# First attention: keys and values for two heads from one weight chunk, four heads' made ahead, heads written out

## What is computed

```python
q, c_kv, k_rope, q_idx, k_idx, w_idx, q_mem = split_cols(h @ w_in, A_SPLITS)
# 8 heads of 128 (96 without, 32 with rotary positions), c_kv of rank 256, sequence 512
c_kv = rmsnorm(c_kv, kv_norm)
# in dsa_attention, by blocks of 128 queries:
dots = jnp.einsum('bqhd,bsd->bqhs', q_idx, k_idx)          # 16 indexing heads of 64
score = jnp.einsum('bqhs,bqh->bqs', jax.nn.relu(dots), w_idx)
_, idx = lax.top_k(jnp.where(causal, score, -inf), topk)   # 128 of at most 512 keys
s = (q_nope @ w_uk . c_kv[idx] + q_rope . k_rope[idx]) * scale
o = softmax(s) @ c_kv[idx]                                 # per head
out = einsum('bshr,rhv->bshv', o, w_uv)
```

## Time and profile before

| what | value |
|---|---|
| median of 3 runs | 2329.89 us (2325.2 to 2333.39) |
| profiled execution, its own time | 2322.4 us |
| its span, first to last instruction | 2320.6 us |
| mean granted TensorE clock | 0.973 of full |
| TensorE busy (matmuls) | 2196.7 us, 95% |
| VectorE busy | 1284.8 us, 55% |
| ScalarE busy | 879.0 us, 38% |
| GpSimd busy | 194.8 us, 8% |
| DMA issues of the weight stream | 334 of 512 KB, 3.5 us to landing |
| chain that ended last | TensorE 84%, VectorE 8%, issue 3%, ScalarE 3%, DMA 1% |

### The profile page before, as it was taken

The page is one execution under the profiler, slowest core; times in us unless marked ns, Lnnn a source line. Parts: engine busy times, 40 slices in busy tenths (PEclk is TensorE's granted clock), DMA queues, the critical chain, the costliest instruction groups (busy, mean ns, idle before and its releaser), DMA issues.

```text
span 2320.6 us, 32126 instructions
## 1 busy us (share of the span) xinstructions
PE 2196.7 (95%) x10706; PEld 1789.9 (77%) x10706; DVE 1284.8 (55%) x2274; ACT 879.0 (38%) x1654; POOL 194.8 (8%) x110
## 2 busy tenths in 40 slices
PE   7986999999999899999999999999999987999997
PEld 6675877888888778788888888888888765777776
DVE  5876444666644546556666445555554474366653
ACT  4443444333222246633333332222222354355541
POOL 0032220100001111110000121000000100000002
PEclk9997999999999999999999999999999998999989
DMA  3121111323333311123233333332332233200002
GB/s 136 54 82 55 64 64 46 100 90 99 99 99 101 92 44 37 37 82 99 91 100 98 104 102 96 97 99 92 97 99 91 90 109 100 64 19 19 19 10 73
DMA packets 50046, 182.90 MB, mean 79 GB/s; under 512 B 5552, under 2 KB 5680, under 8 KB 49840
## 3 DMA queue, kind: packets, MB, share of 16 engines
q1 hardware_dynamic: 49824, 181.35, 24.8%
q0 software_dynamic: 144, 0.52, 0.1%
HBM read 179.76 MB, written 2.10 MB: 78 GB/s over the span
## 4 chain that ended last, share of the span: by engine, by line
PE 84%; DVE 8%; issue 3%; ACT 3%; DMA 1%; POOL 0%; DVEq 0%; ACTq 0%; POOLq 0%; SPq 0%
PE pj L2030 69%; PE po L2316 3%; PE ps L2276 2%; PE po L2215 2%; PE ps L2169 2%; PE pt L2291 2%; ACT w_both L683 1%; PE pt L2185 1%; DVE w_both L1215 1%; DVE rtmp L1345 1%; PE pj L2140 1%; PE ps L2408 1%; DMA raw<-in_wstream 1%; DVE score L1785 1%; PE po L2224 1%
## 5 line engine op out<-in xcount | busy, mean ns | idle before, releaser
L2030 PE MATMUL pj<-h_hi,w_both 128*128 128x512 f32 x3472 | 1134.0, 399 | 26.3 <-DVE w_both L1215 18.8
L2030 PEld LDWEIGHTS pj<-h_hi,w_both 128*128 128x128 f32 x3472 | 657.9, 189 | 165.5 <-issue 17.2
L683 ACT ACTIVATE w_both<-raw 128x1024 fp32r<-128x1024 f32 x334 | 353.9, 1060 | 864.8 <-PE pj L2030 855.1
L2030 PE MATMUL pj<-h_lo,w_both 128*128 128x512 f32 x1736 | 680.4, 392 | 0.0
L1215 DVE TENSOR_TENSOR w_both<-raw,w_both 128x1024 fp32r<-128x1024 f32 x296 | 400.2, 1352 | 386.7 <-ACT w_both L683 386.4
L2030 PE MATMUL pj<-G_hi,w_both 128*128 128x512 f32 x1408 | 440.0, 393 | 3.1 <-DVE G_lo L1442 3.0
L2030 PEld LDWEIGHTS pj<-h_lo,w_both 128*128 128x128 f32 x1736 | 329.6, 190 | 63.9 <-issue 1.4
L2030 PEld LDWEIGHTS pj<-G_hi,w_both 128*128 128x128 f32 x1408 | 266.9, 190 | 63.1 <-DVE G_lo L1442 3.8
L2030 PE MATMUL pj<-G_lo,w_both 128*128 128x512 f32 x704 | 275.9, 392 | 0.0
L2030 PEld LDWEIGHTS pj<-G_lo,w_both 128*128 128x128 f32 x704 | 133.3, 189 | 27.3
L601 POOL TENSOR_TENSOR ssum<-sq 128x512 f32<-128x512 f32 x6 | 9.4, 1562 | 1396.7 <-ACT sq L892 1396.7
(11 more groups left out here) (315 smaller groups left out, 2395.2 us busy)
## 6 DMA issues: line engine op xcount, KB each, us to landing
raw<-in_wstream SPq DMA_DIRECT2D x334, 512.0 KB, 3.5
xT<-in_x SPq DMA_DIRECT2D x4, 512.0 KB, 9.4
out_x<-xT SPq DMA_DIRECT2D x4, 512.0 KB, 2.7
memT<-in_mem SPq DMA_DIRECT2D x1, 1024.0 KB, 12.5
cst<-in_cst SPq DMA_DIRECT2D x1, 512.0 KB, 10.7
tab<-in_tab POOLq DMA_DIRECT2D x1, 512.0 KB, 4.9
posi<-in_pos SPq DMA_DIRECT2D x1, 256.0 KB, 2.8
vec<-in_vec SPq DMA_DIRECT2D x1, 182.5 KB, 2.4
```

The source lines that it names most:

```text
L683: nc.scalar.activation(w_hi[:, c.par * CW:(c.par + 1) * CW], raw[:, c.par * CW:(c.par + 1) * CW], ACT.Copy).then_inc(hi_ready, 1)
L2030: mm = nc.tensor.matmul(acc, w[:, col:col + P], x[part], start=first and k == 0, stop=last and k == 2)
```

## The change

- The stage `aq` has 14 chunks instead of 18: q0, q1, kv0, kv1, q2, q3, q4, kv2, q5, q6, kv3, q7, q8, q9. A `kv` chunk has keys and values of two heads: 4 key blocks, and 4 value blocks in the order in which the two heads' 128 columns lie side by side. The number of uses of the `pj` banks stays 26 (a pair takes four).
- TensorE's `pair_keys` makes the keys of two heads (12 matmuls of 512 columns), `pair_values` their values in 24 matmuls of 256 columns, two token blocks to a bank.
- Pairs 0 and 1 (heads 0 to 3) and query 2 are made before the first scores. Pair 2 is made in head 2, pair 3 in head 4: keys at unit 0, values at unit 1. The query of head j + 3 is made in head j (j up to 6): in pieces of 6 matmuls at each unit, or of 9, 9 and 6 at units 1 to 3 in heads 2 and 4. Head 7 makes nothing.
- ScalarE takes each head's keys when they are done (`pair_done`), then the two halves of the values, and splits one chunk behind each pair and one behind each query. The keys' copies stand ahead of the exponential of unit 2, the values' copies and the split ahead of that of unit 3.
- `a_k` holds four heads and `a_v` two pairs, over memory that the indexing and `ckv` are done with; `rope_key` copies the rotated rows four times.
- `attention_tiles` has no hardware loop for `aq`.

```diff
@@ -38,7 +38,7 @@
 
-STAGES = [("afront", 2), ("idx", 8), ("ckv", 2), ("mem", 8), ("aq", 18), ("aout", OUT_CHUNKS), ("up0", 2 * FT),
+STAGES = [("afront", 2), ("idx", 8), ("ckv", 2), ("mem", 8), ("aq", 14), ("aout", OUT_CHUNKS), ("up0", 2 * FT),
           ("down0", DT * DOWN_CHUNKS), ("bfront", 4), ("bq", 8), ("bmem", 2), ("bout", OUT_CHUNKS), ("up1", 2 * FT),
@@ -58,6 +58,12 @@
           "nz0", "nz1", "cmp2", "nz2", "nz3", "nz4", "nz5", "nz6", "nz7"]
+AQ = ["q0", "q1", "kv0", "kv1", "q2", "q3", "q4", "kv2", "q5", "q6", "kv3", "q7", "q8", "q9"]
+AQ_TILE, _t = {}, 0
+for _name in AQ:
+    AQ_TILE[_name] = TL["aq"] + _t
+    _t += 4 if _name[:2] == "kv" else 1
+assert _t == dict(TILES)["aq"] and len(AQ) == dict(STAGES)["aq"]
 TAKES = {"c": 0, "cmp": 2}
@@ -323,7 +329,8 @@
 
-    a_k, a_v = put("a_k", 2 * S, at=g0 + 20 * KB), put("a_v", 2 * S, at=g0 + 24 * KB)
+    a_k = put("a_k", 4 * S, at=g0 + 20 * KB)
+    a_v = [put("a_v0", 2 * S, at=g0 + 36 * KB), put("a_v1", 2 * S, at=g1 + 38 * KB)]
     c_hi, c_lo = put("c_hi", 2 * S, f32r, at=g0 + 28 * KB), put("c_lo", 2 * S, f32r, at=g0 + 32 * KB)
@@ -514,6 +522,10 @@
 
+            if ph.name == "aq":
+                for j in range(ph.tiles):
+                    tile(ph, 0, j)
+                return
             tile(ph, 0, 0)
@@ -569,18 +581,13 @@
                 return At(CH[ph.name] + j, i, 2), At(TL[ph.name] + j, i, 2)
-            if isinstance(i, int) and j < 2:
-                return At(CH["aq"] + j), At(TL["aq"] + j)
-            if isinstance(i, int) and j == ph.tiles + 1:
-                return At(CH["aq"] + 17), At(TL["aq"] + 25)
-            return At(CH["aq"] + 2 * j, i, 4), At(TL["aq"] + 3 * j, i, 6)
-
-        def keys_values_at(i, j):
-
-            if isinstance(i, int) and j == 0:
-                return At(CH["aq"] + 2), At(TL["aq"] + 2)
-            return At(CH["aq"] + 1 + 2 * j, i, 4), At(TL["aq"] + 1 + 3 * j, i, 6)
-
+            return At(CH["aq"] + AQ.index(f"q{j}")), At(AQ_TILE[f"q{j}"])
+
+        def pair_at(n):
+
+            return At(CH["aq"] + AQ.index(f"kv{n}")), At(AQ_TILE[f"kv{n}"])
+
+        PAIR_IN = {2: 2, 4: 3}
 
@@ -741,12 +748,26 @@
 
-            def keys_values(i, j):
-
-                c, t = keys_values_at(i, j)
-                par = j % 2
-                take(a_k[0:96, par * S:(par + 1) * S], t, c, rows=slice(0, 96))
-                take(a_v[:, par * S:(par + 1) * S], t + 1, c)
+            def pair_keys(n):
+
+                t = pair_at(n)[1]
+                for hh in range(2):
+                    at = (n % 2 * 2 + hh) * S
+                    act.wait_ge(pair_done, 3 * n + hh + 1)
+                    nc.scalar.activation(a_k[0:96, at:at + S], pj[(t + hh).par][0:96, :],
+                                         ACT.Copy).then_inc(pj_free[(t + hh).par], 1)
+
+            def pair_values(n):
+
+                c, t = pair_at(n)
+                for part in range(2):
+                    if part:
+                        act.wait_ge(chunk_used, c.v + 3)
+                    else:
+                        act.wait_ge(pair_done, 3 * n + 3)
+                    nc.scalar.activation(a_v[n % 2][:, part * S:(part + 1) * S], pj[(t + part).par][:, :],
+                                         ACT.Copy).then_inc(pj_free[(t + part).par], 1)
+                split_hi(c + 2)
 
@@ -798,18 +819,16 @@
                         query(ph, i, j + 2)
-                    if ph.name == "aq" and u == 1 and more(ph, i, j):
-                        keys_values(i, j + 1)
+                    if ph.name == "aq" and j in PAIR_IN and u < 2:
+                        (pair_keys, pair_values)[u](PAIR_IN[j])
                     if u == ph.at_refill and more(ph, i, j):
 
-                        if ph.name == "aq":
-                            split_hi(keys_values_at(i, j + 1)[0] + 2)
-                        elif ph.name == "bmem" or ph.name != "amem" and not (isinstance(i, int) and j == 0):
+                        if ph.name == "bmem" or ph.name == "bq" and not (isinstance(i, int) and j == 0):
                             split_hi(query_at(ph, i, j + 1)[0] + 2)
                     softmax(ph, i, j, u + 2)
-                    if u == ph.at_query and ph.name == "aq":
-                        query(ph, i, j + 2)
-                        split_hi(query_at(ph, i, j + 2)[0] + 2)
+                    if u == ph.at_query and ph.name == "aq" and j < ph.tiles - 1:
+                        query(ph, i, j + 3)
+                        split_hi(query_at(ph, i, j + 3)[0] + 2)
                     last = before(ph, i, j, p)
@@ -821,8 +840,11 @@
                 if name == "aq":
-                    keys_values(0, 0)
-                    split_hi(keys_values_at(0, 0)[0] + 2)
+                    for n in range(2):
+                        pair_keys(n)
+                        pair_values(n)
+                    query(ph, 0, 2)
+                    split_hi(query_at(ph, 0, 2)[0] + 2)
                 if name == "bmem":
@@ -1724,8 +1746,8 @@
                 link(rope(ktmp[:, 0:S], vraw[:, :], tab128, SHUF128, t))
-                for par in range(2):
-                    nc.vector.tensor_copy(a_k[96:P, par * S:(par + 1) * S], ktmp[96:P, 0:S])
+                for slot in range(4):
+                    nc.vector.tensor_copy(a_k[96:P, slot * S:(slot + 1) * S], ktmp[96:P, 0:S])
 
@@ -2122,23 +2144,32 @@
 
-            def keys_values(i, j):
-
-                c, t = keys_values_at(i, j)
+            def pair_keys(n):
+
+                c, t = pair_at(n)
                 arrived(c)
-                free(t)
-                for k in range(2):
-                    product(pj[t.par][:, :], k, c.par, (c_hi[:, k * S:(k + 1) * S], c_lo[:, k * S:(k + 1) * S]),
-                            k == 0, k == 1)
-                free(t + 1)
-                acc = pj[(t + 1).par]
+                for hh in range(2):
+                    free(t + hh)
+                    for k in range(2):
+                        mm = product(pj[(t + hh).par][:, :], 2 * hh + k, c.par,
+                                     (c_hi[:, k * S:(k + 1) * S], c_lo[:, k * S:(k + 1) * S]), k == 0, k == 1)
+                    mm.then_inc(pair_done, 1)
+
+            def pair_values(n):
+
+                c, t = pair_at(n)
                 for b in range(NB):
+                    at = t + 2 + b // 2
+                    if b % 2 == 0:
+                        free(at)
                     for k in range(2):
-                        col = c.par * CW + (2 + k) * P
+                        col = c.par * CW + (4 + 2 * k) * P
                         here = slice(k * S + b * P, k * S + (b + 1) * P)
-                        for n, (x, w) in enumerate(((c_hi, w_hi), (c_hi, w_lo), (c_lo, w_hi))):
-                            mm = nc.tensor.matmul(acc[:, b * P:(b + 1) * P], x[:, here], w[:, col:col + P],
-                                                  start=k == 0 and n == 0, stop=k == 1 and n == 2)
+                        for m, (x, w) in enumerate(((c_hi, w_hi), (c_hi, w_lo), (c_lo, w_hi))):
+                            mm = nc.tensor.matmul(pj[at.par][:, b % 2 * 2 * P:(b % 2 + 1) * 2 * P], x[:, here], w[:, col:col + 2 * P],
+                                                  start=k == 0 and m == 0, stop=k == 1 and m == 2)
+                    if b == 1:
+                        mm.then_inc(pair_done, 1)
                 mm.then_inc(chunk_used, 1)
@@ -2152,13 +2183,13 @@
                     if branch in ("mem", "topk"):
-                        q = query_at(ph, i, j)[1] if branch == "mem" else keys_values_at(i, j)[1] + 1
+                        q = query_at(ph, i, j)[1] if branch == "mem" else pair_at(j // 2)[1] + 3
                         pe.wait_ge(pj_free[q.par], q.half + 2)
...
                 if branch == "topk":
-                    keys = a_k[:, par * S:par * S + w]
+                    keys = a_k[:, j % 4 * S:j % 4 * S + w]
                 elif branch == "mem":
@@ -2206,7 +2237,7 @@
                     if branch == "topk":
-                        val = a_v[:, j % 2 * S + kb * P:j % 2 * S + (kb + 1) * P]
+                        val = a_v[j // 2 % 2][:, (2 * kb + j % 2) * P:(2 * kb + j % 2 + 1) * P]
                     elif branch == "mem":
@@ -2234,11 +2265,13 @@
 
-                    if ph.name == "aq" and u == 0 and more(ph, i, j):
-                        keys_values(i, j + 1)
+                    if ph.name == "aq" and j in PAIR_IN and u < 2:
+                        (pair_keys, pair_values)[u](PAIR_IN[j])
                     if ahead(ph, i, j):
-                        if ph.name == "aq" and u:
-                            query(ph, i, j + 2, (range(0, 3), range(3, 6), range(6, CB))[u - 1])
+                        if ph.name == "aq" and j < ph.tiles - 1:
+                            pieces = ((), range(0, 3), range(3, 6), range(6, CB)) if j in PAIR_IN else (
+                                range(0, 2), range(2, 4), range(4, 6), range(6, CB))
```

(28 more changed lines are left out.)

1 line of the change is left out of this document (added).

## The result

The changed kernel took **2306.42 us** (median of 4 runs, 2304.8 to 2310.26) beside 2331.34 us for the kernel before (4 runs): ratio 0.990, 95% interval 0.9876 to 0.9923. The size of the gain, about 1%, is known less well than these medians make it look. With twelve executions of a later group the kernel before has 2324.4, 18.0 above 2306.42; in another group it has 2328.8 (15 executions), and the changed kernel, run again beside it, 2305.86: 22.9. The two profiled executions (2322.4 and 2305.13) are 17.3 apart. So the gain is 17 to 25 us, and the profiles account for the 17. Forecast were -15.6 and 2314.3, in a range of 2305 to 2325.

The account below looks back on a forecast made before the run. VectorE's top-k was taken to bound until about 211 us, TensorE after it. Thin heads -17.0, pair heads +4.9, last head -4.3 and key copies +0.8 give -15.6 us, from the median 2329.9 to 2314.3; range 2305 to 2325.

Parts of the forecast that it names:

- no new waits: Rival: rope and exponentials come in time in the heads, TensorE is the only bound; 2307.4 us, chance 0.12.
- The bound: First attention: VectorE's top-k bounds until about 211 us, TensorE after it.
- The front: Pairs 0, 1 and query 2 before the first scores end near 205 us, hidden by the top-k; first turn stays at 211.
- my sign of being wrong, "after 212": A first turn of the first attention after 212 us would show the forecast wrong.
- Thin heads: Heads 0, 1, 3, 5, 6 without key and value work: 4.0 less, 0.65 rope wait; -3.4 each, -17.0 us.
- Pair heads: Heads 2 and 4, each making a pair: +1.65 of matmuls and 0.8 of waits, +2.45 each, +4.9 us.
- The rival that 256 columns cost twice 128: Value matmuls save nothing by pairing: +2.4 in each of two pair heads, 2319.2 us, chance 0.05.
- The last head: Query work gone from the last head, up to the memory attention's first waiting score: -3.2 - 1.1 = -4.3 us.
- Key copies: Two more key copies of 0.42 us on VectorE at 80 us delay the top-k: +0.8 us.
- rope takes over: Rival: GpSimd's subtraction blocks both rope halves, 1.4 us more in five heads; 2321.3 us, chance 0.10.
- front not covered: Rival: TensorE stays at 1.2 GHz from 187 us, first turn at 219; +8, 2322.4 us, chance 0.10.
- clock drops in the thin heads: Rival: TensorE's clock drops at both waits of seven heads, 26 us slower; 2340 us, chance 0.04.

Follow-up runs that it names:

- rounds_ahead_before: Kernel before, with the product `rck` made by GpSimd and two top-k rounds moved ahead of the norm of `ckv`: 2317.08 us, ratio 0.9957.
- pair1_in_head0: Changed kernel with pair 1 made in head 0 instead of in front of the first scores: 2310.58 us, ratio 0.9935.
- rope_ahead: Changed kernel with VectorE roping query j + 2 in units 2 and 3 of head j, not query j + 1 in units 0 and 1: 2301.35 us.
- exp_first: Changed kernel with ScalarE's exponentials ahead of a pair's copies and split in heads 2 and 4: 2310.8 us, ratio 0.9921.
- before_again: Kernel before, not edited, run and profiled again: 2324.37 us, ratio 0.9991.
- all_together: Changed kernel with the edits of exp_first, rope_ahead and rounds_ahead_after together: 2297.05 us, ratio 0.9869.
- rounds_ahead_after: Changed kernel, with the product `rck` made by GpSimd and two top-k rounds moved ahead of the norm of `ckv`: 2309.25 us, ratio 0.9904.

## Why the prediction was right, and where its terms were off

**The total.** The measured 2306.42 lies inside the range, but 7.9 under the forecast and 1.4 above the range's lower end, next to the rival *no new waits* (2307.4). By the total alone one would have chosen that rival, though the waits that it denies are all there. What carries the forecast is the lengths of the stretches below; that the total fell where it did is in part luck, of TensorE's clock in two places and of the group of runs that the kernel before was measured in.

**The bound.** TensorE after 211, the top-k before it: right. That the top-k alone set the first turn was argued in the forecast and is now shown by rounds_ahead_before. That the product `rck` was not in its way, where the profile put a wait of 9 us, was learned by the two runs that moved it for nothing.

**The front.** "All this is hidden and the first turn stays at 211": hidden it is, by pair1_in_head0. The first turn, at 212.03, is 1.0 later and so touches my sign of being wrong, "after 212"; but none of that comes from the front: the profiled execution was 1.5 late when it split the memory at the start, lost 1.9 more in the indexing stage, and won 2.3 back up to the bias. I had the front end at 205 with a slow first stretch; it ended there at full clock, after a wait of 0.6 for GpSimd's first low half. TensorE's stop at 184 to 186 us, which I took over from the kernel before, did not come, and the clock stayed at 1.00; the stop was an accident of that one profile. The cover was judged too thick: I compared TensorE's end (205) with VectorE's (210) and left out the 2.8 us of ScalarE between the two, the table load among them. It made no difference to this change, but it did to every later step that leaned on it.

**Thin heads**, forecast -3.4 each: -3.1. The wait for the rope shows as 0.65 (forecast 0.65) but costs 0.90, by rope_ahead. Head 0 gave only 2.5 between the first two profiles, since its first six query matmuls ran at half clock and took 2.56 us; between the second two it gave 4.5: there the same place took 2.56 us in the kernel before (six key matmuls) and 1.56 in the changed one. So five heads gave -14.9 or -16.9 instead of -17.0. In the first pair this is the largest term and the largest error. What of the error is not the clock's is the 0.25 us a head that the rope's stop costs beyond its length.

**Pair heads**, forecast +2.45 each and 19.2 us: +2.53 and 19.33. The waits for the exponentials are worth 0.89, by exp_first, forecast 0.8. The 24 value matmuls take 2.89 (forecast 2.9). The rival that 256 columns cost twice 128 is out: it would have had 5.3 us here. It came from the isolated figures (134 and 262 cycles) in the Trainium skill's "TensorE: Matmul & The Clock Gate", section "Back-to-back issue gap". The same section says that they do not hold for a stream of weight loads and matmuls, which is what this kernel has, and gives 81 ns for 128 columns and 131 for 512 there. So the section, read whole, doesn't make 256 columns twice as dear as 128. In these rows, each matmul with a weight load of its own, 128 columns cost 0.111 and 256 cost 0.120 us. More columns cost little more here too, but 128 of them cost 0.111 us and not 0.081, and the measurement decides.

**The last head**, forecast -4.3: from its first value matmul to the memory attention's first masked score 12.83 before (330.73 to 343.56) and 8.74 after, -4.1. No experiment took this term apart.

**Key copies**, forecast +0.8. The two further copies of 0.42 us are there. The indexing stage took 72.7 us before and 74.6 after, but it took 73.9 in before_again, with no copy more and a granted clock of 0.83 from 84 to 94 us. The changed kernel's first profile has 0.83 there too. Between these two the copies are worth 0.7. Two other profiles have their slow stretch elsewhere, at 122 to 126 us: rounds_ahead_before without the further copies (clock 0.61, the stage 73.4) and all_together with them (0.63, 74.9), 1.5 apart. So between 0.7 and 1.5; the forecast's 0.8 lies in it.

Together the heads gave -13.8 (-15.8 in the second pair of profiles) where -15.6 less the 0.8 of the copies, -16.4, were forecast. That the spans of the first pair are nonetheless 17.2 apart, 1.6 better than forecast, is luck of the clock and one lasting effect: the memory attention. In the kernel before, TensorE's clock fell there in all five profiles of that kernel and its variants (0.57 to 0.63 over 4 us, PE busy 3.7 of them); in the changed kernel and its variants it fell in none of nine (1.00, PE busy 2.75). The attention takes 24.2 to 24.5 us in the former and 22.6 to 23.1 in the latter. I had named no gain there. The windows behind the first attention, of the kernel before

```profile
343.80:347.80 4.00, 3.73 (x13) 2.80 (x14) 2.31 (x12) 3.00 (x9) 1.14 (x1) 0.57 0.38 116
```

and of the changed one:

```profile
329.80:333.80 4.00, 2.75 (x16) 1.63 (x15) 2.94 (x12) 2.65 (x9) 0.00 (x0) 1.00 0.00 0
```

Why it keeps its clock was not tried apart: the work ahead of the stop has changed, and so has the length of the stop. The rivals *no new waits*, *rope takes over*, *front not covered* and *clock drops in the thin heads* all have an answer in the rows above: the waits are there, one half of the rope and not both is held up, the first turn comes 1.3 us behind the bias as before, and the granted clock over the heads is 0.99.

## What to carry to other kernels

Work moved under a wait is free up to the time at which the *slowest queue behind it* is ready, not up to the end of the wait that the stopped engine shows: here 6.2 us of idle TensorE were 3.4 us of cover (3.5 by rounds_ahead_after), because a copy, a split and a table load stood on another engine in between. A wait in the middle of a queue costs only if what follows it is needed sooner than the next wait allows; move rounds of the bounding loop into the gap before attacking what ends it. And when filler work is taken out, the order of the small jobs that it hid (a rope, an exponential behind copies) has to be set anew: here that was worth a further 5 us.

## What the runs showed of the chip

- TensorE's granted clock falls to half at a few fixed places in some executions of a program and not in others. At 50 to 60 us it was 0.50 in five of nine profiles of the changed kernel and its variants, for 5.4 to 5.9 us each time, and in none of five of the kernel before and its variants; whether that is chance, so few profiles don't tell. In the last attention, whose code no edit touched, the stretch from the first score with the keys `n_ks` to the first with `n_kw` took 11.2 us in all five profiles of the kernel before and its variants, and in four of nine of the others; 8.5 in the five that are left. These steps are as large as the effects under study. A stretch between two marks in the profile, not the total, is what told 0.9 us a head apart.
- The same stop of TensorE, 1.7 us for VectorE at the start of that attention, was followed by a clock of 0.52 in the profile before and of 1.00 in the profile after:

```profile
2018.00:2024.00 6.00, 6.00 (x15) 2.72 (x16) 1.36 (x6) 3.55 (x10) 0.00 (x0) 0.52 0.19 76
```

```profile
2004.00:2010.00 6.00, 5.87 (x32) 3.58 (x33) 2.96 (x13) 5.25 (x14) 0.00 (x0) 1.00 0.25 84
```

  (windows of the kernel before and of the changed one). Matmuls just ahead of it were the same, busy 4.00 of 4 us. No run here says what decides.
- In fp32r a matmul of 256 columns costs a twelfth more than one of 128 when each brings its own weights: 0.120 against 0.111 us, 2.89 us for 24 and 5.31 for 48.
- VectorE's product of two tiles in memory takes 0.68 us for 128x512 when GpSimd is idle (rope_ahead), and took 2.25 with GpSimd subtracting beside it. Where the two met, TensorE waited 0.65 to 0.67 us in four heads and 0.33 in head 0. GpSimd's subtraction and the first half of the rope in the thin head shown above:

```profile
261.47 2.38 POOL L634 TENSOR_TENSOR w_both<-raw,w_both 128x1024 fp32r<-128x1024 f32 x1 [6.26 <-ACT w_both L690]
262.16 2.25 DVE L1363 TENSOR_TENSOR qs<-qn,tab 128x512 f32<-128x512 f32 x1
```
